# A gated three-branch block and a second block on one core: the recurrence's forget inputs and queries as crossed 512-column products

## Chip, cores and metric

One core of one Trainium2 chip runs the whole program. The metric is the device time of one execution in microseconds, lower is better.

## What is computed

The input is 256 tokens of width 1024. Two transformer blocks follow each other; the change lies in the first mixer of the first block, a recurrence (HGRN2) whose inputs are four slices of one projection of the normed input:

```python
h = _rmsnorm(x, norm_mix_g[l])
z = h @ w_in[l]                       # hq, hf, hi, hg, then the other branches and the gates
f = lb + (1.0 - lb) * sigmoid(f_logit)          # f_logit = hf, lb = softmax of the bounds
qh, kh, ih = heads(silu(q)), heads(1.0 - f), heads(i)     # q = hq, i = hi
G = cumsum(heads(log(f)))
...
o = _rmsnorm(o, norm_g) * silu(g_out)           # g_out = hg
```

`hf` and `hq` are each a 1024 by 512 weight, applied to 256 tokens. Every product is wanted at about float32 accuracy.

## The kernel before

Five engines each run a hand-written program (`pe_program`, `act_program`, `dve_program`, `pool_program`, `sp_program`), and meet only at semaphores. Within an engine everything runs in the order in which it is written; there is no scheduler.

**Weights.** `weight_plan` cuts all weights into numbered units of at most 128x2048 (1 MB). SyncE loads unit i into one of three `raw` buffers once VectorE has finished the unit that lay there (`load`, L2392 to L2395). ScalarE copies it to `Wh`, rounded to fp32r (`hi_to`, L1083; at most NS = 3 units ahead of TensorE, by `unit_end`), and VectorE writes the remainder raw - Wh to `Wl` (`lo_to`, L1574), which raises `w_lo`. In both programs `begin(key)` means: do these conversions up to two units past `key`, here and now in this engine's order. Units 0 and 1 are `hg`, 2 and 3 `hf`, 4 and 5 `hq`, 6 and 7 the two halves of `hi`, 8 and 9 the first gate projection. The turned and normed-gain input lies in `hT`: high parts in columns 0 to 2047, low parts (`hTl`) in the rest.

**Products.** A product a·b is the sum ah·bh + ah·bl + al·bh. `three` (L410) issues these three one after the other for each of the eight 128-row slices k. `rows_out` uses it for a unit of 256 outputs with the weights as the stationary operand: two groups m of 8 x 3 matmuls of 256 columns (the tokens), both groups in one PSUM bank. The feed-forward stages already have another form, `wide` (L417) and `narrow` (L421): the high weight times high and low tokens side by side, 512 columns, and then the low weight times the high tokens, 256 columns; the two halves of the bank must be added afterwards.

**The start of the recurrence.** TensorE's order is: `hg` (L622), `hf` unit 0, `hf` unit 1, `hq` unit 0 (with `spread(0)`, L541, between its groups: it spreads the tokens' root-mean-square factors over all partitions), `hq` unit 1, then `hi`, whose two units are passed in order by `toks_halves`: each half begins with a wait for `w_lo` of its unit. The first gate projection follows in the same way. Between halves of the gate projections lie the recurrence's level products (`own_products`, L664; `level_products`, L674).

VectorE takes `hf` and `hq` from PSUM by one multiply with the tokens' factors `RB` (`rows_scaled`, L1666). ScalarE takes their sigmoids (L1175, L1179), VectorE multiplies q with its sigmoid (L1716). Between them stand `lo_to` of units 5, 6 and 7. Then come the bounds' softmax on columns of 4 (L1719 to L1730, with one exponential on ScalarE, L1181), the sum of the lambdas (L1732, exponential L1183), and f = sigmoid · (1 - lb) + lb (L1738), and the conversions of units 8 and 9.

Of the kernel before, what the change touches and what calls it, by code (L numbers as in the profile page):

```python
# [9 lines left out]
ACT = mybir.ActivationFunctionType  # L10
# [134 lines left out]
def build(nc, plan, I, out):  # L145
    ctx = ExitStack()
    with ctx:
# [45 lines left out]
        ff_hi, ff_lo, x0_hi = sem("ff_hi"), sem("ff_lo"), sem("x0_hi")  # L193
        xt_hi, xt_lo, mt_hi, mt_lo = (sem(n) for n in ("xt_hi", "xt_lo", "mt_hi", "mt_lo"))
# [94 lines left out]
        at = tiles.at  # L289
# [60 lines left out]

        def yT_at(k):
            return yTh[:, k * 256:k * 256 + 256], yTl[:, k * 256:k * 256 + 256]
# [38 lines left out]
        def pe_program(pe):  # L391
# [52 lines left out]
            def rows_out(key, banks, mid=None):  # L444
                i, b = U[key], banks.take()
                t = take(key, b)
                weights(i)
                for m in range(2):
                    ins = three(t[:, m * 256:m * 256 + 256], weight_left(i, 256, m * 128), right(hT_at),
                                EIGHT, True, True)  # L450
                    if m == 0 and mid:
                        mid()
                ins.then_inc(ps_full[b], 1)
                unit_end[i] = full(key)

# [184 lines left out]
            i, b = U["hf", 0], T.take()  # L640
            t = take(("hf", 0), b)
            for m in range(2):
                for n, ks in enumerate((EIGHT[0:4], EIGHT[4:8])):
                    if m == 0:
                        pe.wait_ge(*((w_lo, i + 1) if n else (w1_lo, 1)))
                    ins = three(t[:, m * 256:m * 256 + 256], weight_left(i, 256, m * 128), right(hT_at), ks, n == 0, n == 1)
            ins.then_inc(ps_full[b], 1)
            unit_end[i] = full(("hf", 0))

            rows_out(("hf", 1), T)  # L650
            rows_out(("hq", 0), T, mid=lambda: spread(0))
            rows_out(("hq", 1), WF)
# [418 lines left out]
        def act_program(act):  # L1071
# [64 lines left out]

            rs0, mrs = stat[0][1], mstat[1]
# [15 lines left out]
            hi_to(U["hq", 0])  # L1153
            act.wait_ge(x_in, 16)
            squares(0, 1)
            squares(0, 0)
            hi_to(U["hq", 1])
            act.wait_ge(rstd_made, 1)
            for m in range(2):
                for c in (1, 0):  # L1160
                    t, x = bank[at["hg", m, c][0]], m * 512 + c * 256
                    act.wait_ge(*full(("hg", m, c)))
                    if c:
                        act.activation(ffx[:, 8 * m:8 * m + 8], t[:, 256:264], ACT.Copy,
                                       scale=rs0[:, m:m + 1]).then_inc(*seq.next())
                    act.activation(Sg[:, x:x + 256], t[:, 0:256], ACT.Copy, scale=rs0[:, m:m + 1]).then_inc(*emptied(("hg", m, c)))
            hi_to(U["hi", 0])
            for m in range(2):
                for c in range(2):
                    act.wait_ge(*free(("hg", m, c)))  # L1170
                act.activation(P[m][:, :], Sg[:, m * 512:m * 512 + 512], ACT.Sigmoid).then_inc(g_sig, 1)
            for u in range(2):
                s = E0[:, u * 512:u * 512 + 512]
                act.wait_ge(*free(("hf", u)))
                act.activation(s, s, ACT.Sigmoid).then_inc(f_sig, 1)  # L1175
            for u in range(2):
                begin(("hq", u))
                act.wait_ge(*free(("hq", u)))
                act.activation(E1[:, u * 512:u * 512 + 512], Q[:, u * 512:u * 512 + 512], ACT.Sigmoid).then_inc(q_sig, 1)  # L1179
            act.wait_ge(lb_sub, 2)  # L1180
            act.activation(lbe, lbe, ACT.Exp).then_inc(lb_exp, 1)  # L1181
# [382 lines left out]
        def dve_program(dve):  # L1564
# [96 lines left out]

            def rows_scaled(dst, key, scale=None):
# [37 lines left out]
            dve.wait_ge(c_in, 16)  # L1700
            norm_end(0)
            lo_to(U["hq", 1])
            spread_out(0)
            for u in range(2):
                rows_scaled(E0[:, u * 512:u * 512 + 512], ("hf", u))
            lo_to(U["hi", 0])
            for m in range(2):
                s = Sg[:, m * 512:m * 512 + 512]
                dve.wait_ge(g_sig, m + 1)
                dve.tensor_tensor(s, s, P[m][:, :], ALU.mult).then_inc(g_made, 1)  # L1710
            for u in range(2):
                begin(("hq", u))
                s = Q[:, u * 512:u * 512 + 512]
                rows_scaled(s, ("hq", u))
                dve.wait_ge(q_sig, u + 1)
                dve.tensor_tensor(s, s, E1[:, u * 512:u * 512 + 512], ALU.mult).then_inc(q_made, 1)  # L1716
# [5 lines left out]
            dve.tensor_tensor(lbe[:, 4:8], L1, lbm, ALU.subtract).then_inc(lb_sub, 1)  # L1722
            dve.wait_ge(lb_exp, 1)
# [7 lines left out]
            dve.wait_ge(lam_mul, 2)  # L1731
            dve.tensor_reduce(lams, lamp.rearrange("p (a b) -> p a b", a=2), AXX, ALU.add).then_inc(lam_sum, 1)  # L1732
            dve.wait_ge(*seq.now())
# [5 lines left out]

# [769 lines left out]
```

## Time and profile before

| | |
|---|---|
| runs, median of 3 | 947.79 us (947.78 to 948.12) |
| the profiled execution | 948.22 us |
| its span | 946.4 us |
| TensorE busy | 939.1 us (99%) |
| VectorE busy | 686.3 us (73%) |
| ScalarE busy | 518.8 us (55%) |
| GpSimd busy | 76.0 us (8%) |
| granted TensorE clock, mean | 0.998 of full speed |

Times within the program are counted from the start of the span. A row's first number is the start, the second how long the row lasts from its first instruction's start to its last one's end; successive instructions of one engine overlap a little, so the distance between two starts is the cost in a full queue. TensorE's ends are modelled, so its starts are what to read.

### The profile page before, as it was taken

Reading aid. Unit: us, or ns where it says so; the run is one execution under the profiler, and the core shown is the slowest. Engines: PE = TensorE matmul, PEld = TensorE weight load, DVE = VectorE, ACT = ScalarE, POOL = GpSimd, SP = SyncE. Lnnn points to the kernel's source line nnn. Section 1 sums busy time; section 2 is a strip of 40 time slices with the busy share of each in tenths; the row PEclk is TensorE's granted clock in tenths of the full one; section 3 lists DMA queues with packets and bytes.
Section 4 is the critical chain, followed back from the end, with each engine's and each line's share of the span. In section 5 each row is a group of like instructions: output and inputs, shape, how many; then the busy total and the mean of one; then the engine's idle time right before and its main releaser. Section 6 shows DMA issues by size and latency. Waiting matters only on the chain.

```text
span 946.4 us, 13932 instructions
## 1 busy us (share of the span) xinstructions
PE 939.1 (99%) x5616; PEld 810.4 (86%) x5616; DVE 686.3 (73%) x985; ACT 518.8 (55%) x657; POOL 76.0 (8%) x149
## 2 busy tenths in 40 slices
PE   9999999999999999999999999999999999999997
PEld 9988887788888888888888888889898888888886
DVE  6788667877868777788876757578678677576675
ACT  6776766555356556555655445356546465354554
POOL 1010228171100000000000000000002000000000
PEclk9999999999999999999999999999999999999999
DMA  9844555343565454556364555654534446646451
GB/s 355 333 157 161 175 185 216 134 151 132 187 246 180 172 196 169 220 178 222 137 233 165 198 203 178 222 178 138 201 128 159 156 140 217 222 148 224 162 178 45
DMA packets 26112, 175.11 MB, mean 185 GB/s; under 512 B 3256, under 2 KB 3520, under 8 KB 6080
## 3 DMA queue, kind: packets, MB, share of 16 engines
q1 hardware_dynamic: 25168, 170.15, 50.6%
q10 hardware_dynamic: 880, 4.07, 1.2%
q8 instruction: 45, 0.74, 0.3%
q14 instruction: 19, 0.16, 0.0%
HBM read 173.15 MB, written 1.06 MB: 184 GB/s over the span
## 4 chain that ended last, share of the span: by engine, by line
PE 98%; DMA 1%; DVE 0%; ACT 0%; SPq 0%; issue 0%; ACTq 0%
PE ps L410 52%; PE ps L417 25%; PE ps L421 13%; PE ps L523 1%; PE ps L753 1%; PE ps L769 1%; DMA FP<-in_first 1%; PE ps L804 1%; PE ps L622 1%; PE ps L674 1%; PE ps L818 0%; PE ps L734 0%; PE ps L784 0%; PE ps L541 0%; PE ps L701 0%; PE ps L853 0%
## 5 line engine op out<-in xcount | busy, mean ns | idle before, releaser
L1574 DVE TENSOR_TENSOR Wl<-raw,Wh 128x2048 fp32r<-128x2048 f32 x151 | 345.9, 2293 | 38.0 <-ACT Wh L1083 37.4
L1083 ACT ACTIVATE Wh<-raw 128x2048 fp32r<-128x2048 f32 x154 | 294.3, 1913 | 38.2 <-PE ps L410 34.0
L417 PE MATMUL ps<-hT,Wh 128*128 128x512 f32 x1056 | 247.9, 390 | 0.0
L417 PEld LDWEIGHTS ps<-hT,Wh 128*128 128x128 f32 x1056 | 197.1, 188 | 40.2 <-issue 0.2
L410 PE MATMUL ps<-Wh,hT 128*128 128x512 f32 (+1 forms) x640 | 200.8, 386 | 0.0
L410 PEld LDWEIGHTS ps<-Wh,hT 128*128 128x128 f32 x640 | 118.3, 188 | 24.5 <-issue 1.9
L1417 ACT ACTIVATE Am<-ps 128x512 f32<-128x512 f32 x66 | 39.1, 593 | 178.5 <-PE ps L421 176.3
L421 PEld LDWEIGHTS ps<-hT,Wl 128*128 128x128 f32 x1056 | 132.4, 192 | 3.4
L421 PE MATMUL ps<-hT,Wl 128*128 128x256 f32 x1056 | 133.4, 283 | 0.0
L1659 DVE TENSOR_TENSOR PT<-ps,Am 128x256 f32<-128x256 f32 x132 | 49.7, 418 | 108.1 <-ACT Am L1417 107.9
L410 PE MATMUL ps<-Wh,yTh 128*128 128x512 f32 (+1 forms) x314 | 123.1, 392 | 0.0
L410 PE MATMUL ps<-Wl,yTh 128*128 128x512 f32 (+1 forms) x314 | 122.2, 389 | 0.0
L410 PE MATMUL ps<-Wh,yTl 128*128 128x512 f32 (+1 forms) x314 | 121.9, 388 | 0.0
L410 PE MATMUL ps<-Wl,hT 128*128 128x512 f32 (+1 forms) x320 | 121.5, 380 | 0.0
L410 PE MATMUL ps<-hT,Wh 128*128 128x256 f32 x384 | 70.5, 285 | 0.0
L410 PEld LDWEIGHTS ps<-Wh,yTl 128*128 128x128 f32 x314 | 59.0, 188 | 12.4
L410 PEld LDWEIGHTS ps<-Wl,hT 128*128 128x128 f32 x320 | 60.4, 189 | 10.2
L410 PEld LDWEIGHTS ps<-Wh,yTh 128*128 128x128 f32 x314 | 59.1, 188 | 11.6 <-issue 0.5
L410 PEld LDWEIGHTS ps<-Wl,yTh 128*128 128x128 f32 x314 | 59.1, 188 | 10.7
L410 PEld LDWEIGHTS ps<-hT,Wh 128*128 128x128 f32 x384 | 59.8, 192 | 0.9 <-issue 0.8
L410 PE MATMUL ps<-hT,Wl 128*128 128x256 f32 x192 | 54.3, 283 | 0.0
L1302 ACT ACTIVATE P<-ps,sm 128x256 f32<-128x256 f32 (+1 forms) x56 | 23.3, 426 | 42.0 <-DVE sm L1915 25.4
(248 smaller groups left out, 805.4 us busy)
## 6 DMA issues: line engine op xcount, KB each, us to landing
raw<-in_units SPq DMA_DIRECT2D x154, 1024.0 KB, 4.8
FP<-in_bias ACTq DMA_DIRECT2D x1, 2048.0 KB, 11.3
FP<-in_first SPq DMA_DIRECT2D x2, 768.0 KB, 8.3
FP<-in_first SPq DMA_DIRECT2D x3, 384.0 KB, 4.9
raw<-in_units SPq DMA_DIRECT2D x2, 512.0 KB, 10.8
X<-in_x SPq DMA_DIRECT2D x1, 1024.0 KB, 17.4
Hn<-in_mem SPq DMA_DIRECT2D x1, 1024.0 KB, 9.0
XT<-in_mem_turned SPq DMA_DIRECT2D x1, 1024.0 KB, 11.0
```

The costliest lines, as they stand in the source:

```text
L410: ins = pe.matmul(o, l(k), r(k), start=first and k == ks[0] and j == 0, stop=last and k == ks[-1] and j == 2)
L417: pe.matmul(o, lh(k), hT_both(k), start=first and k == ks[0], stop=False)
L421: ins = pe.matmul(o[:, 256:512], ll(k), hT_at(k)[0], start=False, stop=last and k == ks[-1])
L523: ins = pe.transpose(t[:, q * 128:q * 128 + 128], src[:, m * n + k * 128:m * n + k * 128 + 128], ident)
L622: ins = pe.matmul(ts[m][c][:, 0:z - a], x[:, m * 128:m * 128 + 128], w[:, k, a:z], start=begin, stop=end)
L674: ins = pe.matmul(t[x:x + w, q * w + w - z:q * w + w], s[:, x:x + w], s[:, x + a:x + a + z], start=True, stop=True)
L753: ins = pe.matmul(ts[j][:, x:z], q[ROW[j], c + m * 128:c + m * 128 + 128], k[ROW[j], c:c + z - x], start=True, stop=True)
L1083: act.activation(wh[j % NS][:, 0:n], raw[j % NR][:, 0:n], ACT.Copy).then_inc(w_hi, 1)
L1302: act.activation(P[i % 2][:, x:z], t[:, x:z], ACT.Exp, bias=mn[:, c], scale=-1.0, accum_out=den[:, c]).then_inc(*(emptied(key) if m else s ...
L1417: act.activation(v3(crossed_out(n)), t, ACT.Copy).then_inc(cross_made, 1)
L1574: dve.tensor_tensor(wl[j % NS][:, 0:n], raw[j % NR][:, 0:n], wh[j % NS][:, 0:n].bitcast(F32), ALU.subtract).then_inc(w_lo, 1)
L1659: dve.tensor_tensor(d[:, m, :], t[:, m, :], v3(crossed_out(n))[:, m, :], ALU.add).then_inc(*emptied((key, key + ("x",))[m]))
```

## The change

It does four things.

1. `hf` and `hq` are made by crossed products: for each of the two groups m, 8 matmuls of 512 columns and 8 of 256, each group in a bank of its own (`crossed_rows`; for `hf` unit 0 the same written out with its half-unit waits). TensorE's first wait of a unit is for the high part alone.
2. ScalarE copies each of the eight banks to SBUF (`keep_front`), into `G`, `Vm`, `Iv` and `K`, which are not in use yet, and frees the bank.
3. VectorE adds the two halves there, and multiplies the sum by `RB` in a second operation (`front_rows`), in place of `rows_scaled`.
4. The bounds' softmax moves ahead of the norm's statistics on VectorE and its exponential ahead of unit 5's conversion on ScalarE; the gate's arithmetic (L1738 before) moves from behind both q's to ahead of them, and the lambdas' sum stays behind q.

```diff
+            def crossed_rows(key, banks, mid=None):
+                i = U[key]
+                for m in range(2):
+                    b = banks.take()
+                    t = take(key + (m,), b)
+                    if m == 0:
+                        pe.wait_ge(w_hi, i + 1)
+                    wide(t, weight_left(i, 256, m * 128)[0], EIGHT, True)
+                    if m == 0:
+                        weights(i)
+                    narrow(t, weight_left(i, 256, m * 128)[1], EIGHT, True).then_inc(ps_full[b], 1)
+                    if m == 0 and mid:
+                        mid()
+                unit_end[i] = full(key + (1,))
...
-            rows_out(("hf", 1), T)
-            rows_out(("hq", 0), T, mid=lambda: spread(0))
-            rows_out(("hq", 1), WF)
+            crossed_rows(("hf", 1), T)
+            crossed_rows(("hq", 0), T, mid=lambda: spread(0))
+            crossed_rows(("hq", 1), T)
...
+            def keep_front(key, m):
+                act.wait_ge(*full(key + (m,)))
+                act.activation(front_kept(key)[:, m * 512:m * 512 + 512], bank[at[key + (m,)][0]][:, :],
+                               ACT.Copy).then_inc(*emptied(key + (m,)))
...
             hi_to(U["hq", 0])
+            keep_front(("hf", 0), 0)
             act.wait_ge(x_in, 16)
             squares(0, 1)
             squares(0, 0)
+            keep_front(("hf", 0), 1)
+            act.wait_ge(lb_sub, 2)
+            act.activation(lbe, lbe, ACT.Exp).then_inc(lb_exp, 1)
+            keep_front(("hf", 1), 0)
             hi_to(U["hq", 1])
...
+            keep_front(("hf", 1), 1)
             hi_to(U["hi", 0])
+            keep_front(("hq", 0), 0)
...
             for u in range(2):
                 begin(("hq", u))
-                act.wait_ge(*free(("hq", u)))
+                if u:
+                    keep_front(("hq", 1), 0)
+                keep_front(("hq", u), 1)
+                act.wait_ge(front_made, u + 3)
                 act.activation(E1[:, u * 512:u * 512 + 512], Q[:, u * 512:u * 512 + 512], ACT.Sigmoid).then_inc(q_sig, 1)
-            act.wait_ge(lb_sub, 2)
-            act.activation(lbe, lbe, ACT.Exp).then_inc(lb_exp, 1)
             act.wait_ge(lam_sum, 1)
             act.activation(lams, lams, ACT.Exp).then_inc(lam_exp, 1)
...
+            def front_rows(dst, key):
+                n, d, r = FRONT.index(key), v3(dst), front_kept(key)[:, :].rearrange("p (m s n) -> p m s n", m=2, s=2)
+                for m in range(2):
+                    dve.wait_ge(*free(key + (m,)))
+                dve.tensor_tensor(d, r[:, :, 0, :], r[:, :, 1, :], ALU.add).then_inc(front_joined, 1)
+                dve.wait_ge(front_joined, n + 1)
+                dve.tensor_tensor(d, d, by_token(2), ALU.mult).then_inc(front_made, 1)
+                dve.wait_ge(front_made, n + 1)
...
+            for u in range(2):
+                front_rows(E0[:, u * 512:u * 512 + 512], ("hf", u))
+            lo_to(U["hi", 0])
...
+            for u in range(2):
+                begin(("hq", u))
+                s = Q[:, u * 512:u * 512 + 512]
+                front_rows(s, ("hq", u))
+                dve.wait_ge(q_sig, u + 1)
+                dve.tensor_tensor(s, s, E1[:, u * 512:u * 512 + 512], ALU.mult).then_inc(q_made, 1)
+            dve.wait_ge(lam_mul, 2)
+            dve.tensor_reduce(lams, lamp.rearrange("p (a b) -> p a b", a=2), AXX, ALU.add).then_inc(lam_sum, 1)
```

VectorE from the spreading of the factors to the remainder of unit 7, as it stood before (HG is the buffer that holds Q, K, G, E0 and E1):

```order
L1633 COPY RB<-ps 128x256
L1666 TENSOR_TENSOR HG<-ps,RB 128x512 x2
L1574 TENSOR_TENSOR Wl<-raw,Wh 128x2048
L1710 TENSOR_TENSOR Sg<-Sg,P 128x512 x2
L1666 TENSOR_TENSOR HG<-ps,RB 128x512
L1716 TENSOR_TENSOR HG<-HG 128x512
L1574 TENSOR_TENSOR Wl<-raw,Wh 128x2048
```

The same piece in the changed program:

```order
L1673 COPY RB<-ps 128x256
L1706 TENSOR_TENSOR HG<-HG 128x512
L1708 TENSOR_TENSOR HG<-HG,RB 128x512
L1706 TENSOR_TENSOR HG<-Vm 128x512
L1708 TENSOR_TENSOR HG<-HG,RB 128x512
L1614 TENSOR_TENSOR Wl<-raw,Wh 128x2048
L1773 TENSOR_TENSOR Sg<-Sg,P 128x512 x2
L1778 TENSOR_SCALAR HG<-HG,sm 128x256 x4
L1706 TENSOR_TENSOR HG<-Iv 128x512
L1708 TENSOR_TENSOR HG<-HG,RB 128x512
L1784 TENSOR_TENSOR HG<-HG 128x512
L1614 TENSOR_TENSOR Wl<-raw,Wh 128x2048
```

Three operations of 128x512 and the four of the gate's arithmetic now stand ahead of the remainder of unit 7 that did not before.

ScalarE from the conversion of unit 6 to that of units 8 and 9, in the changed program:

```order
L1210 ACTIVATE P<-Sg 128x512 x2
L1214 ACTIVATE HG<-HG 128x512 x2
L1166 ACTIVATE Iv<-ps 128x512
L1221 ACTIVATE HG<-HG 128x512
L1110 ACTIVATE Wh<-raw 128x2048
L1166 ACTIVATE HG<-ps 128x512 x2
L1221 ACTIVATE HG<-HG 128x512
L1223 ACT_TABLE_LOAD
L1223 ACTIVATE sm<-sm 128x2
L1110 ACTIVATE Wh<-raw 128x2048 x2
```

The order of the sigmoids, of the table load and of the conversions of units 7, 8 and 9 is the one before; the copies L1166 are new, and the bounds' exponential is no longer behind the table load.

## Rows read from the trace of the kernel before

**Rows 1.** The page: busy time; the chain by engine; one costly group (busy, mean ns).
```profile
PE 939.1 (99%) x5616; PEld 810.4 (86%) x5616; DVE 686.3 (73%) x985; ACT 518.8 (55%) x657; POOL 76.0 (8%) x149
...
PE 98%; DMA 1%; DVE 0%; ACT 0%; SPq 0%; issue 0%; ACTq 0%
...
L1417 ACT ACTIVATE Am<-ps 128x512 f32<-128x512 f32 x66 | 39.1, 593 | 178.5 <-PE ps L421 176.3
```

**Rows 2.** TensorE's timeline, 17 to 41 us: start, us, line, out<-in, tile, count.
```profile
17.25 0.40 PE L410 MATMUL ps<-hT,Wh 128*128 128x256 f32 x2
...
31.64 0.61 PE L541 MATMUL ps<-diag,ones 128*128 128x128 f32 x4
...
40.72 0.40 PE L410 MATMUL ps<-Wh,hT 128*128 128x512 f32 x1
```

**Rows 3.** TensorE's timeline in a feed-forward stage that already uses crossed products.
```profile
305.42 6.96 PE L417 MATMUL ps<-hT,Wh 128*128 128x512 f32 x30
...
312.68 4.00 PE L421 MATMUL ps<-hT,Wl 128*128 128x256 f32 x32
316.51 0.40 PE L410 MATMUL ps<-Wh,yTh 128*128 128x512 f32 x1
```

**Rows 4.** VectorE's timeline, 28 to 49 us (idle before, and its releaser, in brackets).
```profile
28.36 0.48 DVE L1628 TENSOR_SCALAR diag<-C,sm 128x128 f32<-128x128 f32 x2
29.35 2.29 DVE L1574 TENSOR_TENSOR Wl<-raw,Wh 128x2048 fp32r<-128x2048 f32 x1 [0.51 <-ACT Wh L1083]
32.29 0.42 DVE L1633 COPY RB<-ps 128x256 f32<-128x256 f32 x1 [0.65 <-PE ps L541]
32.75 1.29 DVE L1666 TENSOR_TENSOR HG<-ps,RB 128x512 f32<-128x512 f32 x2
...
36.15 1.28 DVE L1710 TENSOR_TENSOR Sg<-Sg,P 128x512 f32<-128x512 f32 x2
37.36 0.68 DVE L1666 TENSOR_TENSOR HG<-ps,RB 128x512 f32<-128x512 f32 x1
...
40.55 2.29 DVE L1574 TENSOR_TENSOR Wl<-raw,Wh 128x2048 fp32r<-128x2048 f32 x1 [1.12 <-ACT Wh L1083]
42.76 0.68 DVE L1666 TENSOR_TENSOR HG<-ps,RB 128x512 f32<-128x512 f32 x1
...
45.66 0.16 DVE L1724 TENSOR_TENSOR sm<-sm 128x4 f32<-128x4 f32 x1 [0.49 <-ACT sm L1181]
...
46.55 1.54 DVE L1738 TENSOR_SCALAR HG<-HG,sm 128x256 f32<-128x256 f32 x4
48.71 2.29 DVE L1574 TENSOR_TENSOR Wl<-raw,Wh 128x2048 fp32r<-128x2048 f32 x1 [0.63 <-ACT Wh L1083]
```

**Rows 5.** ScalarE's timeline, 27 to 49 us.
```profile
27.40 1.91 ACT L1083 ACTIVATE Wh<-raw 128x2048 fp32r<-128x2048 f32 x1 [1.32 <-DMA raw<-in_units]
...
30.94 1.95 ACT L1083 ACTIVATE Wh<-raw 128x2048 fp32r<-128x2048 f32 x1
...
38.07 0.63 ACT L1179 ACTIVATE HG<-HG 128x512 f32<-128x512 f32 x1 [1.68 <-DVE HG L1666]
38.61 1.90 ACT L1083 ACTIVATE Wh<-raw 128x2048 fp32r<-128x2048 f32 x1
43.47 0.63 ACT L1179 ACTIVATE HG<-HG 128x512 f32<-128x512 f32 x1 [2.96 <-DVE HG L1666]
44.12 1.28 ACT L1181 ACT_TABLE_LOAD   x1
45.42 0.21 ACT L1181 ACTIVATE sm<-sm 128x8 f32<-128x8 f32 x1
...
46.77 3.71 ACT L1083 ACTIVATE Wh<-raw 128x2048 fp32r<-128x2048 f32 x2
```

**Rows 6.** The tile raw, 20 to 60 us: time from a load's issue to its landing.
```profile
DMA to landing us min/median/max: 4.7/6.6/8.0
```

**Rows 7.** The last stretch: us, busy of each engine, granted clock, DMA share.
```profile
940.27:943.00 2.73, 0.00 (x0) 0.00 (x0) 1.98 (x7) 1.71 (x6) 0.00 (x0) 1.00 0.12 46
```

More of the change, by code:

```diff
@@ L193, in build @@
         ff_hi, ff_lo, x0_hi = sem("ff_hi"), sem("ff_lo"), sem("x0_hi")
+        front_joined, front_made = sem("front_joined"), sem("front_made")
         xt_hi, xt_lo, mt_hi, mt_lo = (sem(n) for n in ("xt_hi", "xt_lo", "mt_hi", "mt_lo"))
@@ L349, in crossed_out, with front_kept @@
             return Am[:, n % 2 * 512:n % 2 * 512 + 512]
+        FRONT = (("hf", 0), ("hf", 1), ("hq", 0), ("hq", 1))
+        def front_kept(key):
+            return (G, Vm, Iv, K)[FRONT.index(key)]
         def yT_at(k):
@@ L639, in pe_program @@
             unit_end[U["hg", 0]] = unit_end[U["hg", 1]] = full(("hg", 1, 1))
-            i, b = U["hf", 0], T.take()
-            t = take(("hf", 0), b)
+            i = U["hf", 0]
             for m in range(2):
+                b = T.take()
+                t = take(("hf", 0, m), b)
+                wh_m, wl_m = weight_left(i, 256, m * 128)
+                for n, ks in enumerate((EIGHT[0:4], EIGHT[4:8])):
+                    if m == 0:
+                        pe.wait_ge(*((w_hi, i + 1) if n else (w1_hi, 1)))
+                    wide(t, wh_m, ks, n == 0)
                 for n, ks in enumerate((EIGHT[0:4], EIGHT[4:8])):
@@ L645, in pe_program @@
                         pe.wait_ge(*((w_lo, i + 1) if n else (w1_lo, 1)))
-                    ins = three(t[:, m * 256:m * 256 + 256], weight_left(i, 256, m * 128), right(hT_at), ks, n == 0, n == 1)
-            ins.then_inc(ps_full[b], 1)
-            unit_end[i] = full(("hf", 0))
-            rows_out(("hf", 1), T)
-            rows_out(("hq", 0), T, mid=lambda: spread(0))
-            rows_out(("hq", 1), WF)
+                    ins = narrow(t, wl_m, ks, n == 1)
+                ins.then_inc(ps_full[b], 1)
+            unit_end[i] = full(("hf", 0, 1))
+            crossed_rows(("hf", 1), T)
+            crossed_rows(("hq", 0), T, mid=lambda: spread(0))
+            crossed_rows(("hq", 1), T)
             WF.n = 6
@@ L1173, in act_program @@
                 s = E0[:, u * 512:u * 512 + 512]
-                act.wait_ge(*free(("hf", u)))
+                act.wait_ge(front_made, u + 1)
                 act.activation(s, s, ACT.Sigmoid).then_inc(f_sig, 1)
@@ L1699, in dve_program @@
             lo_to(U["hq", 0])
[L1700 to L1716, printed above, removed]
             L0, L1 = VT[:, ROWS["lb"]:ROWS["lb"] + 4], VT[:, ROWS["lb"] + 4:ROWS["lb"] + 8]
@@ L1722, in dve_program @@
             dve.tensor_tensor(lbe[:, 4:8], L1, lbm, ALU.subtract).then_inc(lb_sub, 1)
+            dve.wait_ge(c_in, 16)
+            norm_end(0)
             dve.wait_ge(lb_exp, 1)
@@ L1730, in dve_program @@
             dve.tensor_scalar(omlb, lb, -1.0, 1.0, ALU.mult, ALU.add).then_inc(*seq.next())
-            dve.wait_ge(lam_mul, 2)
-            dve.tensor_reduce(lams, lamp.rearrange("p (a b) -> p a b", a=2), AXX, ALU.add).then_inc(lam_sum, 1)
-            dve.wait_ge(*seq.now())
+            lo_to(U["hq", 1])
+            spread_out(0)
+            for u in range(2):
+                front_rows(E0[:, u * 512:u * 512 + 512], ("hf", u))
+            lo_to(U["hi", 0])
+            for m in range(2):
+                s = Sg[:, m * 512:m * 512 + 512]
+                dve.wait_ge(g_sig, m + 1)
+                dve.tensor_tensor(s, s, P[m][:, :], ALU.mult).then_inc(g_made, 1)
             for h in range(4):
```

## The prediction

> **What bounds the kernel now.** I read the page first. TensorE is busy 99% of the span and the chain that ended last is TensorE for 98% [rows 1]. VectorE (73%) and ScalarE (55%) matter only where they make TensorE wait. So an edit gains what it takes off TensorE's stream, and it loses what TensorE has to wait for a unit's remainder (`w_lo`). The waits of TensorE itself came second: from 17 us on none is listed, so today every remainder is ready in time. Third came the timelines of the three engines from 17 to 60 us. They show how early each remainder is.
>
> **TensorE's stream.** The stretch from 17.25 to 31.64 us is two and a half units of `three`, 120 products of 256 columns: 14.39 / 120 = 0.120 us each [rows 2]. A unit is 48 of them, 5.76 us, and the four take 23.03 us. Crossed products are in the feed-forward stage of the same trace: 32 wide ones from 305.42 to 312.68, 0.227 us each, and 32 narrow ones to 316.51, 0.120 us each [rows 3]. A unit becomes 16 x 0.227 + 16 x 0.120 = 5.55 us, the four 22.2 us. Both forms stream the same number of columns, so only 64 fixed costs of a matmul go: **-0.85 us** on TensorE. After it `hi` starts at 40.72 - 0.85 = 39.87 [rows 2], and the first gate projection, 48 products of 512 columns later, could start at 50.8. Before it was 40.72 + 48 x 0.227 = 51.6.
>
> **What VectorE and ScalarE now do ahead of units 7 and 8.** I walk the queue forward. A handover between engines costs 0.03 to 0.04 us (copy ended 32.71, multiply began 32.75; multiply ended 38.04, sigmoid began 38.07) [rows 4, 5].
>
> - *ScalarE up to unit 5's conversion.* It sat idle 1.32 us there for the load, until 27.40 [rows 5]. Two copies of a 128x512 bank at 0.59 us [rows 1] and the bounds' exponential (0.21) [rows 5] come to 1.4 us less the overlaps: they just fill the idle time. The third copy stands ahead of the squares and lies beside their load. Cost nothing; uncovered they would cost 0.6 us each. The exponential brings no table load: the order of the changed program has none there, and ScalarE starts with a set that serves it.
> - *Bounds' softmax on VectorE.* The first part is in idle time before the norm's statistics. The second is four dependent operations, each 0.16 us [rows 4] plus a handover, 0.8 us in all, behind the norm's statistics, which end at 28.84 (29.35 less 0.51 idle). Unit 5's remainder starts at 29.48 in place of 29.35: +0.13.
> - *RB.* TensorE reaches `spread` half a microsecond earlier, at 31.12, and its 0.61 us end at 31.73 [rows 2]. The copy starts at 31.77, not 32.29.
> - *`hf`, joined.* Each unit takes two dependent operations in place of one. One of 128x512 is 0.68 us for a PSUM source, and 1.28 for two from SBUF [rows 4], so a pair with its handovers is 1.44. VectorE is through with both at 32.23 + 2.88 = 35.11 (before: 33.95).
> - *Unit 6's remainder, gate of `hg`.* 2.20 us (29.35's kind, successor distance 40.55 to 42.76) and 1.21 (36.15 to 37.36) [rows 4]: 38.5.
> - *The gate's arithmetic, moved ahead.* Four operations lasted 1.54 us [rows 4]; I take 1.4, since GpSimd ran beside them before: 39.9.
> - *`hq` unit 0, joined.* 1.4: 41.3. Before, its one multiply ended at 38.04 [rows 4].
> - *ScalarE.* Its sigmoid and then unit 7's conversion follow: 38.04 to 38.61 before [rows 5], so the conversion starts at 41.9, lasts 1.90, and VectorE's remainder runs from 43.8 to **46.1** (before 40.55 to 42.84).
>
> TensorE wants unit 7 after half of `hi`, at 39.87 + 24 x 0.227 = 45.3. It waits **0.8 us**. Before, it had 3.3 us in hand (46.16 against 42.84).
>
> From unit 7's remainder to that of unit 8 the order is the old one with more in it: join `hq` unit 1 (starts 46.0, 1.4 us), sigmoid 0.63, table load 1.28, the lambdas' exponential 0.2, conversion of unit 8 at 49.5 for 1.9, remainder 2.29 [rows 4, 5]. It ends at **53.7**, where it ended at 51.00. TensorE, ready at 46.1 + 5.45 = 51.6, waits another **2.2 us**. The copies of `hq` unit 1 (2 x 0.59) lie beside unit 7's remainder (2.29): nothing.
>
> Since the gate projection cannot start before its remainder, the two waits and the saving come to one difference: 53.8 - 51.6 = **+2.2 us**. The 0.85 us saved and the first wait of 0.8 us vanish in it.
>
> **Behind it.** Everything on VectorE is late by 2.7 us here against TensorE's 2.2. The first level's factors were ready 1.9 us early (VectorE's last operation for it ended at 61.59 [rows 4], TensorE's first began at 63.54 [rows 2]) and are so still by 1.4. After that each level waits for TensorE again, so nothing adds up. Loads wait for remainders too: unit 8's load is issued with unit 5's remainder, at 31.8, and lands by 8.0 us later at most [rows 6], 39.8 against a conversion at 49.5; unit 9's 45.4 against 51.4. All later stages are TensorE's own stream and shift as they are.
>
> **The sum.** Profiled execution 948.22 + 2.2 = 950.4 us (its span 946.4, 1.8 us less than its time). The median of the runs lies 0.4 below that execution, so 947.79 + 2.2 = **950.0 us**. A change of 0.2%, 1.9 us, is about what a measurement of this kernel can tell from none.
>
> **Where a page speaks.** The load of a table took 1.28 us, began 0.02 us behind the sigmoid (44.10, 44.12) and was followed 0.02 us later by the exponential [rows 5]; no emptying of the pipe shows. The Trainium skill, "ScalarE: Activation LUTs", section "What ACT_TABLE_LOAD costs", adds about 1.38 us of drain to each load, 2.66 us together. By that rule the sum would be 951.4. The trace disagrees, and I take the row.
>
> TensorE has been without a stop from 17 us on, and the change gives it stops of 0.8 and 2.2 us. In the tail it did nothing from 940.27 to 943.00 and its granted clock was still 1.00, the 2.4 GHz level [rows 7]. I expect no fall. The Trainium skill, "TensorE: Matmul & The Clock Gate", section "HAM oscillation — how this bites in real kernels", warns that gaps in a stream of matmuls bring the half clock, which speaks against this change. The stop of the tail in [rows 7] was longer than either of mine and did not lower the clock.
>
> **The rivals.**
> - *The forecast: remainders of units 7 and 8 late.* 950.0; its own range 949.1 to 951.0 (half a microsecond on each of the two chains passes through in full). Chance 0.72. For it: VectorE has no idle time left in the walk from 31.8 to 41.3.
> - *No remainder is late, the shorter stream shows.* 947.79 - 0.85 = 946.9, not slower. The place is unit 8's `w_lo`, the price is the wait. It decides from the point where VectorE's and ScalarE's chain is 3.0 us shorter than I sum it (53.8 against 50.8); between lie 947 to 949. For it: unit 7 had 3.3 us in hand. Against it: unit 8 had only 0.6 (51.0 against 51.6), and three joins and the gate's arithmetic are now ahead of it. Chance 0.14, the part between included.
> - *The lateness goes on.* If the levels or a load miss their places by the missing 0.5 to 1.5 us, each once: 950.5 to 952. For it: 1.4 us in hand at the first level is little. Chance 0.08.
> - *The table load costs twice its row here.* Another 1.28 us [rows 5] between the sigmoid and unit 8's conversion: 951.3. Chance 0.02, since the row shows nothing beside its 1.28.
> - *The clock falls behind the second wait.* Then a half projection of 5.45 us takes twice that: 950.0 + 5.4 = 955.4. Chance 0.04.
>
> **The numbers.** Faster by over 0.2% (below 945.9) would need more than the whole saving: 0.03. Within 0.2% (up to 949.7) lie the second case and the lower fifth of the first: 0.14 + 0.72 x 0.22 = 0.30, and rounding up for an error common to my two chains, 0.33. Slower: 0.64. The range that leaves out 2 in 10 reaches from 948.0, well into the second case, to 951.8, through the third and the fourth.
>
> **What would show it.** In the changed profile TensorE should have a wait for VectorE's remainder in `hi` of about 0.8 us and one before the first gate projection of about 2.2, the first product of `hi` at 39.9 and of the gates at 53.8, and VectorE's remainder of unit 7 starting near 43.8. The four units should last 22.2 us. I am wrong if the list of TensorE's waits has no such entry; if the gates start before 51.6 the walk over VectorE is at fault, if the four units last 23 us the saving is, and if the span grows by more than the start of the gates does, something behind them.

## The result, and the profile after

| | kernel before | changed kernel |
|---|---|---|
| median of 6 runs | 948.01 us (947.78 to 948.43) | 951.21 us (950.10 to 952.71) |
| ratio, 95% interval | | 1.0036, 1.0025 to 1.0046 |
| the profiled execution | 948.22 us, span 946.4 | 950.10 us, span 948.3 |

The change makes the kernel slower by 3.2 us by medians. Its six runs do not lie together: 950.10, 950.28 and 950.34 at a mean granted clock of 0.999, and 952.08, 952.64 and 952.71 at 0.996 to 0.997. The kernel before has no such second group. The profiled execution is one of the lower group.

The page of the changed kernel: busy time, the chain by engine, and the group that holds the matmuls of `three` (now L416).

```profile
PE 938.5 (99%) x5552; PEld 806.4 (85%) x5552; DVE 689.7 (73%) x989; ACT 522.4 (55%) x665; POOL 73.9 (8%) x149
...
PE 96%; DVE 2%; ACT 1%; DMA 0%; issue 0%; ACTq 0%
...
L416 PE MATMUL ps<-Wh,hT 128*128 128x512 f32 (+1 forms) x640 | 201.3, 387 | 2.5 <-DVE Wl L1614 2.4
```

Against [rows 1], 64 matmuls are gone and 0.6 us of TensorE's busy time. The chain that ended last has gained 2% of VectorE and 1% of ScalarE: it now leads through them for a while. The group names the place: 2.4 us of idle time, released by the remainder of a weight unit.

TensorE's timeline of the changed kernel (start, us, line, operation, count, idle before):

```profile
16.73 2.00 PE L423 MATMUL ps<-hT,Wh 128*128 128x512 f32 x8
18.57 1.11 PE L427 MATMUL ps<-hT,Wl 128*128 128x256 f32 x8
19.52 2.00 PE L423 MATMUL ps<-hT,Wh 128*128 128x512 f32 x8
...
30.70 0.61 PE L562 MATMUL ps<-diag,ones 128*128 128x128 f32 x4
...
39.53 0.40 PE L416 MATMUL ps<-Wh,hT 128*128 128x512 f32 x1
...
45.68 0.50 PE L416 MATMUL ps<-Wh,hT 128*128 128x512 f32 x1 [0.52 <-DVE Wl L1614]
...
53.32 0.50 PE L416 MATMUL ps<-Wh,hT 128*128 128x512 f32 x1 [1.90 <-DVE Wl L1614]
```

The first product of `hf` starts 0.52 us earlier than in [rows 2] (16.73 against 17.25); over the 13 executions of which there is a trace this start lies between 16.62 and 17.65 us, whatever the kernel. A group of 16 lasts 2.79 us (16.73 to 19.52). `hi` starts at 39.53, its second half waits 0.52, and the gates start at 53.32 after a wait of 1.90. (The waits in brackets count from the modelled end of the product before.) From the first product of `hf` to the gates it is 36.59 us; before it was 51.6 - 17.25 = 34.35. The difference is 2.24 us.

VectorE's timeline of the changed kernel, the same stretch as [rows 4]:

```profile
28.95 2.29 DVE L1614 TENSOR_TENSOR Wl<-raw,Wh 128x2048 fp32r<-128x2048 f32 x1
31.34 0.42 DVE L1673 COPY RB<-ps 128x256 f32<-128x256 f32 x1
31.80 0.69 DVE L1706 TENSOR_TENSOR HG<-HG 128x512 f32<-128x512 f32 x1
32.53 0.69 DVE L1708 TENSOR_TENSOR HG<-HG,RB 128x512 f32<-128x512 f32 x1
...
34.71 2.29 DVE L1614 TENSOR_TENSOR Wl<-raw,Wh 128x2048 fp32r<-128x2048 f32 x1
36.92 1.28 DVE L1773 TENSOR_TENSOR Sg<-Sg,P 128x512 f32<-128x512 f32 x2
38.12 1.38 DVE L1778 TENSOR_SCALAR HG<-HG,sm 128x256 f32<-128x256 f32 x4
39.42 0.68 DVE L1706 TENSOR_TENSOR HG<-Iv 128x512 f32<-128x512 f32 x1
...
43.33 2.29 DVE L1614 TENSOR_TENSOR Wl<-raw,Wh 128x2048 fp32r<-128x2048 f32 x1 [1.04 <-ACT Wh L1110]
45.54 0.68 DVE L1706 TENSOR_TENSOR HG<-HG 128x512 f32<-128x512 f32 x1
...
50.97 2.29 DVE L1614 TENSOR_TENSOR Wl<-raw,Wh 128x2048 fp32r<-128x2048 f32 x1 [2.36 <-ACT Wh L1110]
```

From 28.95 to 40 us no idle time is listed. The remainder of unit 7 starts at 43.33 (before 40.55, in an execution that began 0.5 us later), that of unit 8 at 50.97 (before 48.71), and ends at 53.26, where TensorE starts at once.

ScalarE's timeline of the changed kernel, ahead of unit 8:

```profile
46.98 0.63 ACT L1221 ACTIVATE HG<-HG 128x512 f32<-128x512 f32 x1 [2.72 <-DVE HG L1708]
47.64 1.28 ACT L1223 ACT_TABLE_LOAD   x1
48.93 0.20 ACT L1223 ACTIVATE sm<-sm 128x2 f32<-128x2 f32 x1
49.04 3.70 ACT L1110 ACTIVATE Wh<-raw 128x2048 fp32r<-128x2048 f32 x2
```

### The profile page after: what moved, and what is told of

Same layout as the page of the kernel before. It is cut to its first block, busy times and chain, and to the rows that moved or that the text cites. A ratio compares the mean times of both kernels' runs of the same rounds, so it can differ in the third digit from the quotient of the medians.

```text
span 948.3 us, 13822 instructions
## 1 busy us (share of the span) xinstructions
PE 938.5 (99%) x5552; PEld 806.4 (85%) x5552; DVE 689.7 (73%) x989; ACT 522.4 (55%) x665; POOL 73.9 (8%) x149
## 4 chain that ended last, share of the span: by engine, by line
PE 96%; DVE 2%; ACT 1%; DMA 0%; issue 0%; ACTq 0%
PE ps L416 49%; PE ps L423 26%; PE ps L427 14%; PE ps L544 1%; PE ps L643 1%; PE ps L780 1%; PE ps L796 1%; PE ps L831 1%; DVE Wl L1614 1%; PE ps L701 1%; ACT Wh L1110 0%; DMA FP<-in_first 0%; PE ps L761 0%; PE ps L845 0%; PE ps L811 0%
## 5 line engine op out<-in xcount | busy, mean ns | idle before, releaser
L423 PE MATMUL ps<-hT,Wh 128*128 128x512 f32 x1120 | 264.0, 390 | 0.0
L423 PEld LDWEIGHTS ps<-hT,Wh 128*128 128x128 f32 x1120 | 208.6, 188 | 42.3 <-issue 0.2
L416 PE MATMUL ps<-Wh,hT 128*128 128x512 f32 (+1 forms) x640 | 201.3, 387 | 2.5 <-DVE Wl L1614 2.4
L427 PEld LDWEIGHTS ps<-hT,Wl 128*128 128x128 f32 x1120 | 141.1, 191 | 4.0
L427 PE MATMUL ps<-hT,Wl 128*128 128x256 f32 x1120 | 142.3, 283 | 0.0
L416 PEld LDWEIGHTS ps<-Wh,hT 128*128 128x128 f32 x640 | 118.3, 188 | 27.7 <-DVE Wl L1614 3.6
L416 PE MATMUL ps<-Wh,yTh 128*128 128x512 f32 (+1 forms) x314 | 123.0, 392 | 0.0
L416 PE MATMUL ps<-Wl,yTh 128*128 128x512 f32 (+1 forms) x314 | 122.2, 389 | 0.0
L416 PE MATMUL ps<-Wh,yTl 128*128 128x512 f32 (+1 forms) x314 | 121.9, 388 | 0.0
L416 PE MATMUL ps<-Wl,hT 128*128 128x512 f32 (+1 forms) x320 | 121.5, 380 | 0.0
L416 PEld LDWEIGHTS ps<-Wh,yTl 128*128 128x128 f32 x314 | 59.0, 188 | 12.4
L416 PEld LDWEIGHTS ps<-Wl,hT 128*128 128x128 f32 x320 | 60.4, 189 | 10.1
L416 PEld LDWEIGHTS ps<-Wh,yTh 128*128 128x128 f32 x314 | 59.1, 188 | 11.6 <-issue 0.5
L416 PEld LDWEIGHTS ps<-Wl,yTh 128*128 128x128 f32 x314 | 59.1, 188 | 10.7
L416 PE MATMUL ps<-hT,Wh 128*128 128x256 f32 x256 | 47.3, 286 | 0.0
L2336 POOL TENSOR_SCALAR sm<-sm 128x8 f32<-128x8 f32 (+3 forms) x8 | 3.7, 468 | 525.2 <-DVE sm L2241 467.7
L1506 ACT ACTIVATE yTh<-PT 128x512 fp32r<-128x512 f32 x33 | 20.8, 632 | 42.1 <-DVE PT L2161 39.0
```

Source lines behind the costliest of these rows:

```text
L416: ins = pe.matmul(o, l(k), r(k), start=first and k == ks[0] and j == 0, stop=last and k == ks[-1] and j == 2)
L423: pe.matmul(o, lh(k), hT_both(k), start=first and k == ks[0], stop=False)
L427: ins = pe.matmul(o[:, 256:512], ll(k), hT_at(k)[0], start=False, stop=last and k == ks[-1])
L1506: act.activation(yTh[:, j % 2 * 512:j % 2 * 512 + 512], g[:, :], ACT.Copy).then_inc(y_hi, 1)
```

## The experiments

Theory A: the joins and the gate's arithmetic make VectorE late with the remainders of units 7 and 8, and TensorE's clock sometimes falls after the stop that this causes. Its rivals are named with each run. Every kernel was run beside the kernel before on the same chip, whose median was 948.09 us in the first and second set and 948.03 in the third. "Group" means a cluster of the kernel's own runs.

**1. The changed kernel again.** No edit.

> The changed kernel once more, unchanged, because its six runs fell in two groups: 950.1 to 950.3 us at a mean granted clock of 0.999, and 952.1 to 952.7 us at 0.996 to 0.997. Theory A (the stops of TensorE sometimes bring the lower clock): again two groups, some 2.3 us apart, the upper one at the lower mean clock, and a profile that falls in the upper group shows a stretch at the 1.2 GHz level shortly after the first gate projection's wait. Rival B (the second group was a passing state of the chip): all runs at about 950.2, or the kernel before shows two groups as well.

Measured: 950.18 us (11 runs). Nine runs are at 949.93 to 950.49 with a clock of 0.998 to 0.999, two at 952.30 and 952.51 with 0.997. The 33 runs of the kernel before beside it lie between 947.60 and 948.67, one group. So the second group is the changed kernel's own. The profile fell in the lower group.

**2. The gate's arithmetic back behind q.**

```diff
-            for h in range(4):
-                z = E0[:, h * 256:h * 256 + 256]
-                if h % 2 == 0:
-                    dve.wait_ge(f_sig, h // 2 + 1)
-                dve.tensor_scalar(z, z, omlb[:, h:h + 1], lb[:, h:h + 1], ALU.mult, ALU.add).then_inc(*seq.next())
             for u in range(2):
                 begin(("hq", u))
...
             dve.tensor_reduce(lams, lamp.rearrange("p (a b) -> p a b", a=2), AXX, ALU.add).then_inc(lam_sum, 1)
+            for h in range(4):
+                z = E0[:, h * 256:h * 256 + 256]
+                if h % 2 == 0:
+                    dve.wait_ge(f_sig, h // 2 + 1)
+                dve.tensor_scalar(z, z, omlb[:, h:h + 1], lb[:, h:h + 1], ALU.mult, ALU.add).then_inc(*seq.next())
```

> The changed kernel with the gate's four operations put back behind both q's. Theory A (what is late is VectorE's chain ahead of the remainders of units 7 and 8, and each microsecond taken off it comes back): in the changed kernel's trace the four operations cost 1.3 us between the gate of hg and the join of hq unit 0. Without them unit 7's remainder ends at about 44.3, before TensorE wants it (no wait in hi), and unit 8's at 52.0 in place of 53.3. The gates start 1.3 us earlier, 948.9 us where the changed kernel has 950.2, with one wait of about 1.4 us left; with stops that short there should be no second group of runs. Rival B (ScalarE's table load and exponential hold unit 8, not VectorE's queue): no gain, 950.2.

Measured: 948.99 us (948.53 to 949.85, 11 runs), ratio to before 1.0010 (1.0002 to 1.0019). TensorE's list has a single wait of 1.4 us; the stop in `hi` is gone. VectorE's timeline of this kernel shows why the four are free here:

```profile
47.60 1.59 DVE L1786 TENSOR_SCALAR HG<-HG,sm 128x256 f32<-128x256 f32 x4
50.05 2.29 DVE L1614 TENSOR_TENSOR Wl<-raw,Wh 128x2048 fp32r<-128x2048 f32 x1 [0.86 <-ACT Wh L1110]
```

They run while VectorE would otherwise wait for ScalarE's conversion of unit 8. Moved forward they stood where VectorE had nothing to spare. That one move costs 1.2 us of the lower group's 2.1. None of the 11 runs is near 951. That alone is weak evidence that the second group is gone: beside it the changed kernel had 2 upper runs of 11, and at that rate none in 11 would still come about one time in nine (an estimate, (9/11)^11 = 0.11).

**3. The moves alone, on the kernel before.**

```diff
             squares(0, 0)
+            act.wait_ge(lb_sub, 2)
+            act.activation(lbe, lbe, ACT.Exp).then_inc(lb_exp, 1)
             hi_to(U["hq", 1])
```

The bounds' softmax and the gate's arithmetic on VectorE stand where the change puts them; products and reads of PSUM are those of before.

> The kernel before with the moves alone: the bounds' softmax and the gate's arithmetic moved forward as in the change, products and reads of PSUM as before. Theory A: the gate's arithmetic makes q 1.4 us later, the softmax moved away from ScalarE's path gives 1.2 of it back, so unit 7's remainder ends at 44.2 (wanted at 46.2) and unit 8's at 51.2 (wanted at 51.6): no wait, 948.0 us, the same as before. Rival B (the moves alone make TensorE wait): 1 us or more above before.

Measured: 948.28 us (947.82 to 948.70), ratio 1.0001 (0.9992 to 1.0010), no wait of TensorE but the first. The moves alone cost nothing that can be told from zero. The joins with the gate's arithmetic behind q cost 0.9 us (experiment 2), both together 2.1: each uses up time in hand that the other then lacks.

**4. The units' conversions first.** The changed kernel, with the conversion of unit 7 ahead of `hq` unit 0's join and that of unit 8 ahead of `hq` unit 1's sigmoid.

```diff
                 keep_front(("hq", u), 1)
+                hi_to(U["hi", 1] + u)
                 act.wait_ge(front_made, u + 3)
...
+                if not u:
+                    lo_to(U["hi", 1])
                 front_rows(s, ("hq", u))
+                if u:
+                    lo_to(U["hi", 1] + 1)
                 dve.wait_ge(q_sig, u + 1)
```

> The changed kernel with the conversions of unit 7 ahead of the join of hq unit 0, and those of unit 8 ahead of hq unit 1's sigmoid, on ScalarE and VectorE. Theory A (the waits for the remainders are the whole loss): unit 7's remainder ends at about 41.6, unit 8's at about 48.9, both ahead of TensorE (45 and 50.5), so both waits go and the 0.85 us of the crossed products show: 947.2 us, 0.8 below before, no second group of runs. The first level's factors have then hardly anything in hand; if they are late it costs up to 0.5. Rival B (the crossed products save nothing here, or the joins cost in other places too): 948.0 or more.

Measured: 947.64 us (946.94 to 948.00, 11 runs). TensorE's list has no wait for a remainder, and there is one group. The gain against before is 0.45 us, less than the 0.85 expected.

**5. A longer stop.** The changed kernel with three multiplies without use ahead of unit 8's remainder.

```diff
+            dve.wait_ge(w_hi, U["hi", 0] + 3)
+            for _ in range(3):
+                dve.wait_ge(*seq.now())
+                dve.tensor_tensor(PT[1][:, :], P[0][:, :], P[0][:, :], ALU.mult).then_inc(*seq.next())
             begin(("hi", 0))
```

> The changed kernel with three dependent multiplies of 128x512 without use (0.7 us each) ahead of unit 8's remainder on VectorE. The arithmetic of the kernel is unchanged. By the walk alone the gates start 2.15 us later and every run takes 950.2 + 2.15 = 952.3. Theory A (the upper group of the changed kernel's runs is the lower TensorE clock after the stop ahead of the gates, more likely the longer the stop): most runs are 2 us or more above 952.3, at about 954.5, at a mean clock of 0.997 or less, and the profile shows a stretch at the 1.2 GHz level behind the stop. Rival B (the upper group has another cause): all runs at 952.3 at a mean clock of 0.999, no such stretch.

Measured: 953.52 to 954.41 us, median 954.10, in all five runs; mean clock 0.997 to 0.998. TensorE's timeline and the windows around the stop (us of the stretch, busy time of PE, PEld, DVE, ACT and POOL, granted clock, DMA share, GB/s):

```profile
56.11 0.50 PE L416 MATMUL ps<-Wh,hT 128*128 128x512 f32 x1 [3.96 <-DVE Wl L1614]
```

```profile
54.00:56.00 2.00, 0.00 (x0) 0.00 (x0) 2.00 (x2) 0.00 (x0) 0.00 (x0) 1.00 0.00 0
56.00:58.00 2.00, 1.89 (x7) 1.52 (x8) 1.97 (x5) 1.80 (x4) 1.11 (x2) 0.80 0.49 74
58.00:60.00 2.00, 2.00 (x6) 1.60 (x5) 2.00 (x2) 2.00 (x4) 1.75 (x1) 0.50 1.00 418
60.00:62.00 2.00, 2.00 (x9) 1.56 (x8) 1.97 (x2) 1.98 (x3) 0.00 (x0) 0.85 0.72 176
```

Every run is above the 952.3 of the walk, by 1.2 to 2.1 us. The stop lasts from 52.15 to 56.11 us. The granted clock is at full speed through all of it, falls to the 1.2 GHz level at 57.2 (read in windows of 0.1 us), 1.1 us after TensorE has resumed and 5.0 us after it stopped, and is back at 60.6. The figure of 954.5 was a little high. That the stop brings the lower clock is what was expected. Only the profiled run shows it directly; for the other four the time and the mean clock speak.

**6. One stop of 2 us.** The kernel of experiment 2 with one such multiply.

> The kernel with the gate's arithmetic put back (one stop of 1.4 us) with one multiply of 128x512 without use ahead of unit 8's remainder: a single stop of 2.0 to 2.1 us ahead of the gates, where the changed kernel has 0.5 and 1.9. By the walk 949.0 + 0.7 = 949.7. Theory A1 (the longest stop decides whether the clock falls): some of the runs, as in the changed kernel 5 of 17, are 2.3 us above that. Theory A2 (the two stops count together): none is.

Measured: seven runs, two at 949.39 and 949.51 with a clock of 0.999, five at 950.97 to 951.90 with 0.997 to 0.998. The profile, from the upper group, has a single wait of 2.04 us and the half level behind it:

```profile
52.00:54.00 2.00, 0.45 (x2) 0.41 (x3) 2.00 (x3) 0.74 (x3) 0.09 (x1) 1.00 0.00 0
54.00:56.00 2.00, 2.00 (x8) 1.62 (x7) 1.97 (x3) 1.99 (x3) 1.58 (x3) 0.70 0.65 193
56.00:58.00 2.00, 2.00 (x6) 1.52 (x6) 2.00 (x2) 2.00 (x4) 1.20 (x1) 0.50 0.79 332
```

So one stop is enough, and A2 (the two stops count together) falls. Here the clock falls at 54.8, 1.2 us after TensorE has resumed (53.55) and 3.3 us after it stopped (51.51), and is back at 58.2. With the first stop absent the share of upper runs was not smaller than in the changed kernel, which beside it had 3 of 5 (experiment 8).

**7. The table load out of the path.** The changed kernel with the lambdas' sum and exponential beside the bounds'.

```diff
             act.activation(lbe, lbe, ACT.Exp).then_inc(lb_exp, 1)
+            act.wait_ge(lam_sum, 1)
+            act.activation(lams, lams, ACT.Exp).then_inc(lam_exp, 1)
```

> The changed kernel with the lambdas' sum and exponential moved up beside the bounds' exponential, so that no table load stands between hq unit 1's sigmoid and the conversion of unit 8. Theory A (a load costs its 1.28 us row and nothing beside): unit 8's conversion starts 1.4 us earlier, the gates start 1.4 us earlier (at the same start of the first product), 948.8 us, with 0.5 us of waiting left ahead of the gates. Rival B (a load costs 2.66 us, drain included): the gates start as soon as TensorE is ready, no wait is left ahead of them, 948.3.

Measured: 949.10 us (948.66 to 949.60, 11 runs, one group), and this stretch of TensorE's and of VectorE's timelines:

```profile
46.26 0.50 PE L416 MATMUL ps<-Wh,hT 128*128 128x512 f32 x1 [0.56 <-DVE Wl L1614]
...
52.38 0.50 PE L416 MATMUL ps<-Wh,hT 128*128 128x512 f32 x1 [0.35 <-DVE Wl L1614]
```

```profile
43.91 2.29 DVE L1614 TENSOR_TENSOR Wl<-raw,Wh 128x2048 fp32r<-128x2048 f32 x1 [1.04 <-ACT Wh L1110]
...
50.03 2.29 DVE L1614 TENSOR_TENSOR Wl<-raw,Wh 128x2048 fp32r<-128x2048 f32 x1 [1.04 <-ACT Wh L1110]
```

From unit 7's remainder to unit 8's it is 6.12 us, where the changed kernel has 7.64 (43.33 to 50.97). The load and the exponential together were worth 1.52 us, not 2.66 or more. ScalarE is not rid of a load by this: one now stands behind the conversions of units 8 and 9, at 51.83 us, and TensorE does not wait for it. A wait ahead of the gates is left, so the rule of a drain beside each load, which the Trainium skill has in "ScalarE: Activation LUTs", "What ACT_TABLE_LOAD costs", does not hold here: 1.28 us for the load and its 0.2 for the exponential are the whole.

**8. The changed kernel a third time.**

> The changed kernel a third time, for the share of its runs that fall in the upper group (5 of 17 so far) and for a profile of one. Theory A: between 1 and 5 of 11 at 952.0 to 952.7 with a mean clock of 0.997 or less, the others at 950.2; a profile in the upper group has a stretch at the 1.2 GHz level behind the stop ahead of the gates. Rival B: none, all at 950.2.

Measured: five runs, 950.08 and 950.40 at 0.998 to 0.999, and 952.25, 952.31 and 952.53 at 0.997. With experiment 1 and the first measurement that makes 8 of 22 runs in the upper group. This time the profile is one of them. Its timeline has the same wait as the lower group's:

```profile
53.97 0.62 PE L416 MATMUL ps<-Wh,hT 128*128 128x512 f32 x1 [1.90 <-DVE Wl L1614]
54.39 0.63 PE L416 MATMUL ps<-Wl,hT 128*128 128x512 f32 x1
54.82 1.05 PE L416 MATMUL ps<-Wh,hT 128*128 128x512 f32 x2
...
57.97 0.39 PE L416 MATMUL ps<-Wl,hT 128*128 128x512 f32 x1
58.19 0.63 PE L416 MATMUL ps<-Wh,hT 128*128 128x512 f32 x2
...
61.27 0.76 PE L691 MATMUL ps<-HG 128*32 128x32 f32 x64
```

The windows of this profile, and then those of experiment 1's, from the lower group:

```profile
50.40:54.00 3.60, 1.70 (x9) 1.08 (x7) 2.37 (x3) 2.99 (x2) 0.73 (x3) 1.00 0.00 0
54.00:57.40 3.40, 3.40 (x9) 2.61 (x10) 3.37 (x4) 3.33 (x6) 2.65 (x3) 0.53 0.68 234
```

```profile
50.40:54.00 3.60, 1.73 (x8) 1.15 (x7) 2.64 (x3) 2.94 (x3) 0.51 (x2) 1.00 0.00 0
54.00:57.40 3.40, 3.40 (x16) 2.76 (x16) 3.37 (x4) 3.38 (x5) 2.86 (x3) 1.00 0.78 263
```

Two executions of the same program with the same stop: in one the clock is 1.00 after it and 16 matmuls are recorded in 3.4 us, in the other it is 0.53 and there are 9. At the half level a product of 512 columns takes 0.43 us (54.39 to 54.82) against 0.23. The clock falls at 54.2, 0.2 us after TensorE has resumed and 2.1 us after it stopped (52.07), and is back at 57.6. The recurrence's own products (L691) stand 24 products behind the first one of the gates. In experiment 1's profile, where the gates start at 53.71, their row is

```profile
59.40 0.76 PE L691 MATMUL ps<-HG 128*32 128x32 f32 x64
```

which is 5.69 us behind the gates' start. Here it is 7.30 (53.97 to 61.27), in the profile of experiment 6 7.26 and in that of experiment 5 7.28. So the low clock costs 1.6 us where a trace can be read. The medians of the two groups of these five runs are 2.1 us apart (952.31 against 950.24); where the other 0.5 us go is not shown. The two profiled executions are 1.8 us apart, 1.6 of it this and 0.26 their different start.

**9. Without the additions.** Only the first half of each bank is taken, in one operation.

```diff
-                dve.tensor_tensor(d, r[:, :, 0, :], r[:, :, 1, :], ALU.add).then_inc(front_joined, 1)
-                dve.wait_ge(front_joined, n + 1)
-                dve.tensor_tensor(d, d, by_token(2), ALU.mult).then_inc(front_made, 1)
+                dve.tensor_tensor(d, r[:, :, 0, :], by_token(2), ALU.mult).then_inc(front_made, 1)
```

> The changed kernel with the addition of the two halves left out in all four joins: only the first half (high weight times high tokens) is taken, in one operation, so the output is not the reference's. Theory A (what made units 7 and 8 late is the second operation of the joins and the gate's arithmetic): 0.73 us less in each join; unit 7's remainder starts 2.2 us earlier, unit 8's 2.9 us earlier and ends at about 50.4, when TensorE is ready for it. At most 0.2 us of waiting is left, the gates start 2.7 to 2.9 us earlier, 947.4 us, one group of runs. Rival B (copies on ScalarE are what is late): less than half of that comes back, 948.8 or more.

Measured: 947.72 us (947.21 to 948.06, 11 runs), no wait of TensorE for a remainder; unit 7's starts at 41.75 and unit 8's at 48.67. ScalarE's eight copies are all still there. Rival B falls: the copies are hidden. What is late is VectorE's extra operation in the joins; the gate's arithmetic, still ahead of `hq` here, brings TensorE no wait without it.

**10. The units first, again.** The kernel of experiment 4, with the same edit.

> The kernel with the units' conversions first, again, against the kernel before on this chip: it was 0.45 us below before by medians, 947.64 against 948.09. Theory A: the crossed products save 0.69 us on TensorE (a group of 16 lasts 2.79 us in place of 2.88, eight groups) and nothing waits: 0.4 to 0.7 us below before. Rival B: no difference.

Measured: 947.42 us (946.89 to 948.03) against 948.03. The mean of the two measurements' 22 runs is 947.54, that of the 60 runs of before beside them 948.12. With a spread of about 0.3 us in each set, the difference of 0.58 us has a standard error of about 0.08. Each measurement's own ratio, 0.9995 (0.9986 to 1.0004), does not exclude no change; both together do, by this working. This version is the fastest of the three, some 0.6 us of 948 below the kernel before.

**11. The units first, and one load less in the path.** The kernel of experiment 4 with the edit of experiment 7.

```diff
             act.activation(lbe, lbe, ACT.Exp).then_inc(lb_exp, 1)
+            act.wait_ge(lam_sum, 1)
+            act.activation(lams, lams, ACT.Exp).then_inc(lam_exp, 1)
```

> The units' conversions first, and the lambdas' sum and exponential beside the bounds', which takes the table load from between q's sigmoid and unit 9's conversion. Theory A (TensorE has no wait left, so what ScalarE and VectorE gain is worth nothing): the same as the kernel with the units first, 947.6. Rival B (the first level still loses something to a late factor): 0.2 to 0.5 us less.

Measured: 947.41 us (946.79 to 948.31), the same as experiment 10's. Unit 9's remainder starts 1.7 us earlier than there (51.09 against 52.79, with TensorE's `spread` 0.35 us later), and nothing comes of it. Where TensorE does not wait, an earlier helper is worth nothing.

## Why the prediction was right, and where it was not

**The walk over VectorE and ScalarE held.** The distance from `hf`'s first product to the gates grew by 2.24 us where the forecast was +2.2, and the lower group's runs (950.10 to 950.34) are the 950.0 us of the sum. The steps, with the changed kernel's times moved by the 0.52 us by which its start was earlier: remainder of unit 5 at 29.47 (29.48 forecast), `hf` joined by 35.2 (35.11), unit 7's remainder at 43.85 (43.8), its end at 46.1 (46.1), unit 8's end at 53.8 (53.7), the gates at 53.84 (53.8). The first wait was 0.52, not 0.8, and the second 1.90, not 2.2: they are listed from the modelled end of the last product, 0.16 us later than the place in the full queue where the next one would have started, and `hi` started 0.2 us later than forecast. The difference of the two starts does not depend on either.

One step does not add up as written. The bounds' four operations, 0.8 us behind 28.84, would end at 29.64, not 29.48. They took 0.68 (28.27 to 28.95, the first of them beginning before the norm's last had ended), so the step's figure was right and its working was not. With 29.64 the sum would have been 0.2 us higher. The first level's times, 61.59 and 63.54, stand in no row that the prediction names; they are shown below.

**The saving on TensorE was 0.7 us, not 0.85.** "16 x 0.227 + 16 x 0.120" took the rate of the wide products from the feed-forward stage [rows 3]. Here eight wide ones last 1.84 us (16.73 to 18.57), 0.230 each, and a group 2.79 us. Five groups last 13.97 (16.73 to 30.70), so eight are 22.35 us against 23.03; from the first product of `hf` to that of `hi` it is 22.80 against 23.47. The forecast of the slower kernel does not depend on it, as the prediction said, but the gain of experiments 4 and 10 does: 0.45 and 0.61 us by medians, where experiment 4 expected 0.85.

**The step that failed is the one on the clock.** The prediction said "I expect no fall", from a stop of 2.73 us in the tail with the clock at 1.00 [rows 7], and gave the rival 0.04 and 5.4 us. The runs: after a stop of 1.90 us the clock fell in 8 of 22 executions, after 2.04 us in 5 of 7, after 3.96 in 5 of 5, and in none of the 22 executions of experiments 2 and 7, whose longest stops are 1.4 and 0.56 us. (The groups are counted by time and mean clock; the fall itself was seen in three profiles, and a stop's length is that of the profiled execution.) The 8 of 22 are 3 of 6, 2 of 11 and 3 of 5 in three measurements, the last two on different chips, so the share at 1.9 us is rough, and that it is smaller than at 2.04 us is not shown.

What was wrong with the step is that its row ends too early. The next two microseconds of the same trace, of the kernel before, with TensorE still at rest:

```profile
943.00:944.00 1.00, 0.00 (x0) 0.00 (x0) 0.20 (x1) 0.17 (x1) 0.00 (x0) 0.77 0.00 0
944.00:945.00 1.00, 0.00 (x0) 0.00 (x0) 0.00 (x0) 0.00 (x0) 0.00 (x0) 0.50 0.96 375
```

(The columns are those of experiment 5.) The clock did fall in that tail, at 943.5, 3.3 us after the end of the last product (940.27). It does so in the tail of all 13 traces, 2.8 to 5.2 us after the last product. The three falls in the middle of the stream came 2.1, 3.3 and 5.0 us after TensorE had stopped. So the fall lags behind the beginning of the stop by an amount that differs from one execution to the next. In the tail it comes while TensorE rests; behind a stop of 2 or 4 us it came when TensorE was at work again. A row that shows 1.00 during a stop therefore does not show that the stop is harmless.

The price was also too high: the half level lasts some 3.4 us in each of the three, not a half projection at half speed throughout, and costs 1.6 us in the traces and 1.8 to 2.4 between the groups of runs. It is that group which lifts the median of the six runs, half of them upper ones, from 950.2 to 951.21. That median lies outside the forecast's own range (949.1 to 951.0) and inside the wider one (948.0 to 951.8). How many runs fall in the upper group varies: in experiment 1 it was 2 of 11, and the median was 950.18.

The same profile taken once could have hidden all of this. The lower group's profile shows clock 1.00 up to the tail; the list of runs gave it away. The Trainium skill, "TensorE: Matmul & The Clock Gate", section "What's actually happening", says that the stretches over which the chip judges TensorE's activity run freely and are not tied to a kernel's start. That the same program with the same stop comes out one way or the other, and that the lag differs, agrees with it; no run here tests it by itself.

**The rivals.** That no remainder is late fell with TensorE's list of waits. That the lateness goes on fell as well: two rows of the kernel before, from which the prediction took its times for the first level's factors,

```profile
60.90 0.69 DVE L1766 TENSOR_TENSOR HG<-HG 128x512 f32<-128x512 f32 x1
```

```profile
63.54 0.76 PE L674 MATMUL ps<-HG 128*32 128x31 f32 x64
```

have these as their counterparts in the changed kernel,

```profile
63.16 0.69 DVE L1813 TENSOR_TENSOR HG<-HG 128x512 f32<-128x512 f32 x1
```

```profile
65.37 0.76 PE L701 MATMUL ps<-HG 128*32 128x31 f32 x64
```

with 65.37 - 63.85 = 1.5 us in hand (forecast 1.4), and no further wait. The table load that costs more than its row fell with experiment 7.

**Where the expected gain went.** Experiments 4 and 10 show that most of it was there. It was covered by a helper's queue: the crossed form takes 0.7 us off TensorE and puts four operations of 0.73 us on VectorE, in a stretch where VectorE and ScalarE had nothing to spare, ahead of the remainder that TensorE wants next; the gate's arithmetic, which had been free behind q, was put there too. With the gate's arithmetic back 1.2 us of the lower group's 2.1 are gone (experiment 2), without the additions or with the units first all of it.

## What to carry to other kernels

Before work is moved between engines or forward in a queue, find what stands behind it in that queue and when the bounding engine wants that; here the slack was 3.3 us for one unit and 0.6 for the next, and the smaller one decided. Put the conversions that the bounding engine waits for first and the work with no reader yet behind them. Even a short stop of a TensorE that was never idle can cost nearly as much again in clock, in some executions only, so read the list of runs and their mean clocks before one profile. And where a row is to show that something does not happen, read on behind its end.

## What was not expected of the hardware

After a stop of 1.9 to 2.0 us in a stream of matmuls the granted clock fell to the 1.2 GHz level in 13 of 29 executions, by their times and mean clocks. Two of these were profiled. The fall came 2.1 and 3.3 us after TensorE had stopped, 0.2 and 1.2 us after it had resumed, and lasted 3.4 us. After a stop of 3.96 us all five runs were slow, and the one profiled had the fall 5.0 us after TensorE had stopped, 1.1 us into the work. The tails of all 13 traces show it 2.8 to 5.2 us after the last product. In the stream it cost 1.6 us by the traces. After 1.4 us it did not come in 11 runs, which is too few to say never.

As forecast, a table load between a sigmoid and an exponential costs its 1.28 us row and nothing beside: 7.64 us became 6.12 when it and the exponential were moved out of the path.
